# More second units by seven products in five feed-forward networks, and their conditioning work spread differently

## The reference, cut to what matters

```python
def _swiglu(h, w_in, w_out):              # D = 1024, hidden 2816
    a, b = jnp.split(h @ w_in, 2, axis=-1)
    return (jax.nn.silu(a) * b) @ w_out

x = x + 0.5 * _swiglu(_rmsnorm(x, norm), w_in, w_out)   # networks 1 to 4 (n = 0 to 3)
x = x + g2 * swiglu(modulate(rms_norm(x, norm2_gain), sh2, sc2), w_ffn_in, w_ffn_out)   # network 5 (n = 4)

mod = jax.nn.silu(c) @ w_ada + b_ada      # conditioning: 1024 x 6144, for c and c_ctx
sh1, sc1, g1, sh2, sc2, g2 = jnp.split(mod, 6, axis=-1)
```

## Time and profile before

| what | value |
|---|---|
| median of 3 runs | 2766.44 us (2766.41 to 2766.52) |
| the profiled execution, its own time | 2765.36 us |
| its span | 2763.70 us |
| TensorE busy | 2742.6 us, 99% |
| VectorE busy | 1892.0 us, 68% |
| ScalarE busy | 1182.6 us, 43% |
| granted TensorE clock | 0.999 of full speed |

### The profile page before, as it was taken

How to read it: one execution, slowest core, us unless ns; L and a number is a source line. 1 busy time by engine, 2 the same in 40 slices (tenths; PEclk the granted TensorE clock), 3 DMA queues, 4 the chain that set the end, 5 groups by cost and what they waited for, 6 DMA issues and landing times. The chain is left out here.

```text
span 2763.7 us, 37768 instructions
## 1 busy us (share of the span) xinstructions
PE 2742.6 (99%) x15532; PEld 2371.2 (86%) x15532; DVE 1892.0 (68%) x2624; ACT 1182.6 (43%) x1431; POOL 39.4 (1%) x77
## 2 busy tenths in 40 slices
PE   9999999999999999999999999999999999999998
PEld 7898887789988899888877899988898988899988
DVE  6998666468895688965665688935555543688843
ACT  5333237453342433423555544524544432444432
POOL 0000000000000000000000000000000000000000
PEclk9999999999999999999999999999999999999999
DMA  4333342123334333343111333234322122223332
GB/s 163 115 130 131 133 139 64 47 99 120 125 122 145 127 110 119 127 139 129 57 51 62 107 104 106 97 107 156 110 78 70 47 77 100 71 104 107 108 107 77
DMA packets 69109, 289.25 MB, mean 105 GB/s; under 512 B 7680, under 2 KB 30336, under 8 KB 40528
## 3 DMA queue, kind: packets, MB, share of 16 engines
q1 hardware_dynamic: 60480, 257.18, 26.9%
q0 software_dynamic: 8032, 29.37, 3.3%
q10 hardware_dynamic: 432, 0.36, 0.0%
HBM read 284.78 MB, written 2.10 MB: 104 GB/s over the span
## 5 line engine op out<-in xcount | busy, mean ns | idle before, releaser
L604 ACT ACTIVATE sb_WH<-sb_RAW 128x2048 fp32r<-128x2048 f32 x238 | 455.4, 1913 | 732.4 <-PE PS L2607 731.7
L2605 PE MATMUL PS<-sb_HH,sb_WH 128*128 128x512 f32 (+1 forms) x2080 | 743.7, 358 | 5.3 <-DVE sb_HL L1474 1.9
L2606 PE MATMUL PS<-sb_HL,sb_WH 128*128 128x512 f32 (+1 forms) x2080 | 737.6, 355 | 0.0
L2607 PE MATMUL PS<-sb_HH,sb_WL 128*128 128x512 f32 (+1 forms) x2080 | 737.4, 355 | 0.0
L1455 DVE TENSOR_TENSOR sb_WL<-sb_RAW,sb_WH 128x2048 fp32r<-128x2048 f32 x185 | 423.2, 2287 | 329.1 <-ACT sb_WH L604 329.1
L2605 PEld LDWEIGHTS PS<-sb_HH,sb_WH 128*128 128x128 f32 x2080 | 393.2, 189 | 66.2 <-issue 3.6
L2607 PEld LDWEIGHTS PS<-sb_HH,sb_WL 128*128 128x128 f32 x2080 | 393.1, 189 | 55.5
L2606 PEld LDWEIGHTS PS<-sb_HL,sb_WH 128*128 128x128 f32 x2080 | 393.3, 189 | 55.2 <-issue 1.4
L2605 PE MATMUL PS<-glh_GHI,sb_WH 128*128 128x512 f32 (+1 forms) x924 | 350.8, 380 | 0.0
L2607 PE MATMUL PS<-glh_GHI,sb_WL 128*128 128x512 f32 (+1 forms) x924 | 350.2, 379 | 0.0
L2606 PE MATMUL PS<-glh_GLO,sb_WH 128*128 128x512 f32 (+1 forms) x924 | 350.1, 379 | 0.0
(11 more groups left out here) (455 smaller groups left out, 4125.0 us busy)
## 6 DMA issues: line engine op xcount, KB each, us to landing
sb_RAW<-in_weights SPq DMA_DIRECT2D x221, 1024.0 KB, 4.9
ff_ADAW<-in_w_ada POOLq DMA_DIRECT2D x48, 512.0 KB, 3.9
sb_RAW<-in_weights SPq DMA_DIRECT2D x39, 512.0 KB, 4.9
out_t<-sb_XT SPq DMA_DIRECT2D x8, 256.0 KB, 2.5
sb_XT<-in_x SPq DMA_DIRECT2D x3, 512.0 KB, 8.7
sb_RAW<-in_weights SPq DMA_DIRECT2D x4, 256.0 KB, 3.7
b_CT<-in_ctx POOLq DMA_DIRECT2D x1, 1024.0 KB, 7.6
hy_BD<-in_c_gates POOLq DMA_DIRECT2D x1, 512.0 KB, 3.3
```

Of the source, the lines that this page charges most:

```text
L604: act.activation(WH[slot][:, :], RAW[slot][:, :], ACT.Copy).then_inc(*T["w_hi"].up())
L2605: pe.matmul(out, wh, xh, start=start, stop=False)
L2606: pe.matmul(out, wh, xl, start=False, stop=False)
L2607: return pe.matmul(out, wl, xh, start=False, stop=stop)
```

## The change

Three tables and three small edits in VectorE's order. Second units by seven products: in networks 1 to 3 now pairs 4, 6 and 8 (none before), in network 4 pairs 2, 3, 5, 6, 8, 9 (before 3, 5, 7, 9), in network 5 pairs 2 to 9 (before 2, 3, 5, 6, 8, 9). Together 13 more. Conditioning in networks 1 to 3: five halves after step `sums_low` of pairs 2, 3, 5, 7, 9 (before eight, pairs 2 to 9), eleven at output units 0 to 10 (before eight, at 1, 2, 4, 5, 7 to 10). Where a second unit by seven products is followed by a plain one, the split of that plain unit moves ahead of the scaling and gating. The transposes in the input stage wait for the gating before them.

```diff
-SEVEN_B = {3: (3, 5, 7, 9), 4: (2, 3, 5, 6, 8, 9)}
-
-ADA_IN = {2: (0, 1), 3: (0, 1), 4: (0, 1), 5: (0, 1), 6: (0, 1), 7: (0, 1), 8: (0, 1), 9: (0, 1)}
-ADA_OUT = {1: 1, 2: 1, 4: 1, 5: 1, 7: 1, 8: 1, 9: 1, 10: 1}
+SEVEN_B = {0: (4, 6, 8), 1: (4, 6, 8), 2: (4, 6, 8), 3: (2, 3, 5, 6, 8, 9), 4: (2, 3, 4, 5, 6, 7, 8, 9)}
+
+ADA_IN = {2: (0, 1), 3: (0, 1), 5: (0, 1), 7: (0, 1), 9: (0, 1)}
+ADA_OUT = {0: 1, 1: 1, 2: 1, 3: 1, 4: 1, 5: 1, 6: 1, 7: 1, 8: 1, 9: 1, 10: 1}
@@ gated(i), VectorE
                     if second:
                         joined(i, 1)
+                        if i < FFN_IN // 2 - 1 and i + 1 not in SEVEN_B[n]:
+                            split(u0 + 2 * i + 3)
                         dve.wait_ge(*q_posts(n, i, 4, 1))
@@ conditioned, VectorE
-                def conditioned(count, bank):
+                def conditioned(count, bank, done):
...
                         if h:
-                            if bank < 4:
-                                dve.wait_ge(T["g_mul"].sem, 22 * n + 22)
+                            dve.wait_ge(T["g_mul"].sem, 22 * n + 2 * done)
                             turned_sums(u - ADA_PER * n + 1, ADA_PER * n - 1, bank)
...
-                    conditioned(ADA_OUT.get(c, 0), 3)
+                    conditioned(ADA_OUT.get(c, 0), 3, 11)
@@ the loop over pairs, VectorE
                     if i in SEVEN_B.get(n, ()):
                         raw_sums(i, 1)
                         sums_low(i, 1)
-                    else:
+                    elif i - 1 not in SEVEN_B.get(n, ()):
                         split(u0 + 2 * i + 1)
...
-                    conditioned(ADA_IN.get(i, (0, 0))[0], 7)
+                    conditioned(ADA_IN.get(i, (0, 0))[0], 7, i)
...
-                    conditioned(ADA_IN.get(i, (0, 0))[1], 7)
+                    conditioned(ADA_IN.get(i, (0, 0))[1], 7, i)
```

## The result

The changed kernel takes 2778.07 us (median of 6 runs, 2776.62 to 2779.40) against 2766.48 of the kernel before on the same chip (2766.41 to 2766.66): ratio 1.0042, 95% interval 1.0032 to 1.0053. It is slower, as forecast, but by 11.6 us where the forecast was 6.9; the median lies 1 us above the range of 2762 to 2777, and two of the six runs (2776.62 and 2776.66) lie inside it.

What follows compares the result with a forecast made beforehand. The prediction took TensorE, 99% busy, as the bound. Waits 16.5 plus restarts 1.3 minus gain 10.9 made 6.9 us slower than the profiled 2765.36; with 1.08 to the median, 2773.3 us, range 2762 to 2777.

Steps and rivals of the forecast that it cites:

- Gain: In all five networks, 13 more units by seven products save 0.84 us of TensorE each: 10.9 us.
- Waits: TensorE waits for late scaling ahead of first units: 12.7 and 1.1 us in networks 1 to 3, 2.7 in network 4.
- Restart: After each of 12 waits the first 256-column matmul costs 0.11 us more: 1.3 us.
- Nothing for the early split, the output stages, the loads: Early split (0.5 us of cover), three halves moved to the output stage, and weight and tile loads: costed at nothing.
- so I add nothing for the clock: A 2.10 us wait in the trace of before kept full clock speed, so the clock was put at nothing.
- the median of the runs is 1.08 above the profiled one: Whole kernel: 1.08 us from the profiled execution to the median of the runs, taking 2772.3 to 2773.3 us.
- Rival 1: TensorE is never held up, VectorE's lateness being absorbed: 2755.5 us, faster; 12 in 100.
- rival 2: Only the long waits of networks 1 to 3 appear, not those of 0.38 and 0.89 us: 2768.9 us; 15 in 100.
- rival 3: A second wait behind the first, at the gating or the early split: +24 us, 2790; 8 in 100.

Runs made afterwards that it cites:

- experiment 6: The changed kernel with the early split undone, so that split again follows scaling and gating: 2776.69 us, 1.0039 to the kernel before.
- Experiment 9: The changed kernel with 16 (in one place 12) matmuls of overwritten result in each of six long waits of networks 1 to 3: 2774.88 us, 1.0035.
- 11: Against the kernel before: seven-product units spread out, conditioning moved, scaling ahead of the next weights, seven useless matmuls in the wait for the keys: 2761.08 us, 0.9984.
- experiment 2: The changed kernel with the input stage's five conditioning halves at pairs 2 (two), 5, 9 and 10 in networks 1 to 3: 2770.29 us, 1.0018.
- 3: The changed kernel with the halves moved as in experiment 2 and the scaling ahead of the next weights' preparation: 2770.08 us, 1.0016.
- 5: The changed kernel with the input stage's five conditioning halves at pairs 2 (two), 3, 5 and 7: 2773.43 us, 1.0027.
- 7: The changed kernel with the conditioning of the kernel before and all the new second units: 2802.75 us, 1.0134.
- 12: The changed kernel with both conditioning halves of pair 2 moved to pair 3, behind its products: 2799.62 us, 1.0124.

## Why the prediction was wrong

The mechanism was right, and almost all of its terms.

- **Gain.** Network 5's stretch became 1.63 us shorter (2 x 0.84 = 1.68 forecast). Held.
- **Waits.** All 12, and none else, where forecast, behind the scaling. From start to start, pair 4 of network 2 takes 691.31 - 668.84 = 22.47 us, 2.33 over two units; 2.12 was forecast. VectorE's chain was off by 0.07 (its end 22.33 us after pair 4's start, 22.26 forecast); the larger part is the hand-over of 0.14, which I had left out. It comes again in every wait. In network 1 the first of them was 1.6 us, not 2.1, and its trace tells why: TensorE had waited 0.44 us for a split one unit earlier, at 86.75, as it did in the kernel before at 86.43, and so started pair 4 later against VectorE's queue. The half ends 4.04 us into pair 4 there, not 4.60.
- **Restart.** The unit behind a wait takes 10.15 us, not 10.07: 0.08 each, 0.11 forecast.
- **Nothing for the early split, the output stages, the loads.** Held: experiment 6, and 111.3 us for each output stage before and after.
- **"A wait of 2.10 us at 2129.39 left the granted clock at full speed, so I add nothing for the clock."** This is the step that failed. It put the clock at nothing on the strength of one wait. The profiled execution had three drops of 1.4 to 1.5 us, 4.4 us together, and experiments 9 and 11 take such drops away by filling the waits.
- **"the median of the runs is 1.08 above the profiled one"**. After the change it was 0.18 below it. The 1.08 was an accident of which execution was profiled: before, that one took 2765.36 us and the runs 2766.41 to 2766.66, and on the third chip these are the lower and the upper of two groups (see 11). That a drop at the wait for the keys makes the difference fits the times; no trace shows it.

With the terms as measured, network 2's stretch is 2 x 2.31 + 0.49 (the waits) + 3 x 0.08 (the restarts) - 3 x 0.84 (the gain) + 1.48 (a drop) = 4.3; it was 4.36. The waits are the idle times that the trace prints, 2.15 and 0.33, with 0.16 added: a matmul of 256 columns is printed with 0.28 us though the next one starts after 0.12, and idle time counts from its printed end. Network 3, with two drops, comes to 5.8; it was 5.84. Network 4 gives 1.5; it was 1.51. So of the 6.0 us between the forecast for the profiled span (2763.7 + 6.9 = 2770.6) and the 2776.6 measured, 4.4 are the clock, 1.0 the waits with their restarts (18.8 against 17.8), 0.3 stand ahead of the first stage, and 0.3 are spread over the rest. Experiment 9 shows the change with no drops: a span of 2772.35 us, 8.65 above the one profiled before, against the 6.9 of the forecast.

The row I argued from was true; the conclusion was not, since one case can't show what happens in some cases only. Counted over the profiles of before, after and all experiments, that very wait for the keys was left unfilled in 13 of them, and in 4 the clock fell behind it. In the input stages 32 waits were 2.1 to 2.3 us long, and 19 of them had a drop (changed kernel 3 of 5, and 1 of 5 the second time; experiment 2, 1 of 1; 3, 1 of 1; 5, 3 of 4; 6, 2 of 5; 7, 6 of 8; 12, 2 of 3). Five waits were 1.86 to 1.89 us, one with a drop. None of the waits of 1.7 us or less had one. Rival 1 (never held up) and rival 2 (only the long waits) are out by the 12 waits; rival 3 (a second wait behind the first) is out, as no gating or split was late.

What stays open is what decides between a drop and none at a wait of 2.2 us. The place in the program does not: at 1048 one execution of the changed kernel had a drop and another none. So it is to be looked for in when a wait falls in an execution; no run here was made to tell.

## What to carry to other kernels

In a kernel that one engine bounds, what a cheaper unit costs the engine that prepares it is paid only where that engine's queue is full: lay out its work from deadline to deadline, with the 0.14 us of the hand-over, and spread such units over the pairs that have room, here every third in place of every second. A wait of TensorE of 2 us may cost 1.5 us more than it lasts, so it is the length of the longest waits, not only their sum, that is to be brought down; where one can't be, matmuls without a use in it keep the clock. One profile in which a thing did not happen is no evidence that it does not: look at the spread of the runs, where steps of one size betray an event that comes and goes.

## What the runs showed of the hardware

In these profiles the granted clock fell to its lower level behind single waits of 1.9 to 2.3 us, in a TensorE that was otherwise nearly always busy, in 24 of 50 cases, always for 3.41 us; behind waits of 6.3 to 7.4 us in three of three, for 6.83 us. A drop of 3.41 us cost 1.4 to 1.5 us. The Trainium skill, page TensorE: Matmul & The Clock Gate, section "HAM oscillation — how this bites in real kernels", tells of a kernel whose clock fell again at each of its waits for a DMA. Here it fell behind 24 of the 50 waits of 1.9 to 2.3 us and behind each of the three of 6.3 to 7.4, so that the time of one program varies from run to run by whole drops.
